# Recurrent layers of a four-layer decoder: sigmoids through ScalarE with a bounded input, one level product a quarter, key products one level ahead

## What is computed

```python
proj = h @ w_in                                   # 1024 x 4096
q, f, i, g = jnp.split(proj, 4, axis=-1)
q = jax.nn.silu(heads(q)); f = heads(f); v = heads(i)      # 8 heads of 128
log_f = jnp.logaddexp(jnp.log(lb), jnp.log1p(-lb) + jax.nn.log_sigmoid(f))
k = (1.0 - lb) * jax.nn.sigmoid(-f)
# o[t] = sum over s <= t of (q[t] . k[s] . prod of exp(log_f) over s < r <= t) v[s]
o = gla_chunkwise(q, k, v, log_f)
o = rmsnorm(o, head_norm)
return (o * jax.nn.silu(g)) @ w_out
```

## Time and profile before

| | us |
|---|---|
| median of three runs (1212.9 to 1214.92) | 1213.76 |
| the profiled execution | 1213.17 |
| its span, first to last instruction | 1211.0 |

### The profile page before, as it was taken

One profiled execution on the slowest core, in us unless ns is written; L12 is line 12 of the kernel. 1 busy time (PEld: TensorE's weight loads), 2 busy tenths in 40 slices (PEclk: granted clock), 3 DMA queues, 4 the chain that ended last, 5 costly groups with the idle time before them and its releaser, 6 DMA issues.

```text
span 1211.0 us, 16960 instructions
## 1 busy us (share of the span) xinstructions
PE 1156.7 (96%) x6750; PEld 1027.2 (85%) x6750; DVE 787.0 (65%) x825; ACT 639.9 (53%) x741; POOL 37.2 (3%) x53
## 2 busy tenths in 40 slices
PE   9778999999999999999999999999876999999998
PEld 8767999888889989888888888888875899888886
DVE  6567778655656676756657866555656787755663
ACT  6544566544454445645556654545653376544553
POOL 1110000000001000000000000000201000000000
PEclk9878999999999999999999999999987999999999
DMA  9322435565455644664654556456422343555450
GB/s 334 106 92 83 139 109 200 179 208 208 162 207 166 199 156 134 205 218 150 218 187 168 181 183 219 152 208 209 138 72 88 105 156 105 174 208 209 151 212 35
DMA packets 85960, 200.82 MB, mean 166 GB/s; under 512 B 3341, under 2 KB 6503, under 8 KB 85904
## 3 DMA queue, kind: packets, MB, share of 16 engines
q1 hardware_dynamic: 85872, 200.01, 48.4%
q0 software_dynamic: 32, 0.03, 0.0%
HBM read 198.95 MB, written 1.08 MB: 165 GB/s over the span
## 4 chain that ended last, share of the span: by engine, by line
PE 80%; DVE 8%; ACT 7%; issue 5%; POOL 0%; DVEq 0%; ACTq 0%; POOLq 0%
PE misc L625 10%; PE hb L625 10%; PE acc L677 10%; PE acc L678 10%; PE acc L679 10%; PE hb L630 5%; PE misc L630 5%; PE hb L569 3%; PE hb L571 3%; PE hb L572 3%; ACT whi L1048 3%; PE acc L832 1%; DVE arena L1661 1%; DVE wlo L1427 1%; PE misc L572 1%
## 5 line engine op out<-in xcount | busy, mean ns | idle before, releaser
L1427 DVE TENSOR_TENSOR wlo<-raw,whi 128x2048 fp32r<-128x2048 f32 x184 | 416.9, 2292 | 185.8 <-ACT whi L1048 184.6
L1048 ACT ACTIVATE whi<-raw 128x2048 fp32r<-128x2048 f32 x183 | 342.4, 1904 | 122.7 <-PE acc L679 104.8
L677 PE MATMUL acc<-whi,arena_r 128*128 128x512 f32 x512 | 199.9, 390 | 0.0
L678 PE MATMUL acc<-wlo,arena_r 128*128 128x512 f32 x512 | 199.5, 390 | 0.0
L679 PE MATMUL acc<-whi,arena_r 128*128 128x512 f32 x512 | 199.2, 389 | 0.0
L569 PE MATMUL hb<-xhl,whi 128*128 128x256 f32 x416 | 128.0, 308 | 7.6 <-DVE gains L1719 4.2
L625 PE MATMUL misc<-xhl,whi 128*128 128x512 f32 x512 | 122.6, 390 | 0.1
L625 PE MATMUL hb<-xhl,whi 128*128 128x512 f32 x512 | 122.7, 390 | 0.0
L571 PE MATMUL hb<-xhl,whi 128*128 128x256 f32 x416 | 122.6, 295 | 0.0
L572 PE MATMUL hb<-xhl,wlo 128*128 128x256 f32 x416 | 122.5, 294 | 0.0
L679 PEld LDWEIGHTS acc<-whi,arena_r 128*128 128x128 f32 x512 | 96.1, 188 | 20.2
(11 more groups left out here) (250 smaller groups left out, 1629.5 us busy)
## 6 DMA issues: line engine op xcount, KB each, us to landing
raw<-in_mlp_w_dram SPq DMA_DIRECT2D x128, 1024.0 KB, 5.4
raw<-in_a_w_in_dram SPq DMA_DIRECT2D x31, 1024.0 KB, 5.4
raw<-in_b_w_qkv_dram SPq DMA_DIRECT2D x12, 1024.0 KB, 6.8
raw<-in_a_w_out_dram SPq DMA_DIRECT2D x8, 1024.0 KB, 5.1
raw<-in_b_w_out_dram SPq DMA_DIRECT2D x4, 1024.0 KB, 5.1
arena<-in_x_dram SPq DMA_DIRECT2D x2, 512.0 KB, 4.6
raw<-in_a_w_in_dram SPq DMA_DIRECT2D x4, 256.0 KB, 4.3
arena<-bias_rows SPq DMA_DIRECT2D x1, 1024.0 KB, 10.8
```

What stands on the lines that cost most here:

```text
L677: pe.matmul(o, ys, h, start=first and kt == 0, stop=False, skip_group_check=True)
L678: pe.matmul(o, ys, l, start=False, stop=False, skip_group_check=True)
L1048: act.activation(whi[:, g % 2, u, 0:n], raw[:, g % 2, u, 0:n], ACT.Copy).then_inc(hi_done, 1)
L1427: dve.tensor_tensor(wlo[:, g % 2, u, 0:n], raw[:, g % 2, u, 0:n], whi[:, g % 2, u, 0:n].bitcast(F32), ALU.subtract).then_inc(lo_done, 1)
```

## The change

- The sigmoids are made by ACT alone, out of exp(-ln(1 + exp(-z))). So that exp cannot overflow, DVE bounds z to 40 in one `tensor_scalar` right behind the evict (`f_bound`, and inside `q_evict` and `gate_evict`). For f ACT makes six activations in one go (`sigmoids`; eight in layer 3), for q and the gate three (`silu`), and one DVE multiply follows for q and gate. The two DVE instructions of `f_b` are gone; those of `silu_a` and `gate_silu_a` became the bound.
- One level a quarter: `level_after` puts level l after quarter l + 3.
- In quarter q DVE first does the queries' product of the next level, then the keys' product of the level after that (one level ahead), then `select`; evictions, silu multiplies and the split follow.
- ACT's splits stand first in every even quarter, DVE's last in every odd one.
- The copy of levels 0 and 8 moves from DVE to ACT (`first_level`).
- PE makes the diagonal products of quad 1 a quarter earlier, the outputs of quad 0 after quarter 13 (before 17), the first sums of squares after 17 (before 20). In layer 0 its wait for the gains stands at level 0 (before: ahead of quarter 0).

The diff, cut:

```diff
+SATURATED = 40.0
...
-        after_quarter = {2: (0,), 3: (1,), 5: (2,), 6: (3,), 8: (4,), 9: (5,), 10: (6,), 11: (7, 8), 12: (9,), 13: (10,),
-                         14: (11,), 15: (12,), 16: (13,), 17: (14,), 18: (15,)}
+        def level_after(quarter):
+            return quarter - 3 if 3 <= quarter <= 18 else None
...
                         group("T", g0 + 1, 2, free, need, first_norm)
-                        pe.wait_ge(gains_sb, 2)
...
+                        elif level == 0 and layer == 0:
+                            pe.wait_ge(gains_sb, 2)
...
-                        pe.wait_ge(bank_free, free_count(layer) + 10)
+                        pe.wait_ge(bank_free, free_count(layer) + 8 + 2 * quad)
...
-                    also = {2: lambda: diagonal_products(0), 11: lambda: diagonal_products(1), 17: lambda: quad_outputs(0),
-                            20: lambda: (quad_outputs(1), oms_step(0), oms_step(1)),
+                    also = {2: lambda: diagonal_products(0), 10: lambda: diagonal_products(1), 13: lambda: quad_outputs(0),
+                            17: lambda: (oms_step(0), oms_step(1)), 20: lambda: quad_outputs(1),
                             22: lambda: (oms_step(2), oms_step(3))}
                     def some_steps(quarters=[0]):
                         if quarters[0] in also:
                             also[quarters[0]]()
-                        for level in after_quarter.get(quarters[0], ()):
-                            level_product(level)
+                        if level_after(quarters[0]) is not None:
+                            level_product(level_after(quarters[0]))
...
-                    def f_a(b):
-                        if b < 2:
-                            act.wait_ge(f_z, 2 * j + b + 1)
...
-                    def f_b(b):
-                        after_dve()
-                        for region in (ff, kq):
...
+                    def sigmoids(b):
+                        act.wait_ge(f_z, 4 * j + b + 1)
+                        z = scratch[b % 2][0].rearrange("p (t x) -> p t x", t=TT)
+                        own = [(bank_of(ff, b), -1.0), (bank_of(kq, b), 1.0)]
+                        for to, sign in own:
+                            ch.did(act.activation(to.rearrange("p t h x -> p t (h x)"), z, ACT.Exp, scale=sign))
...
+                            ch.settle(1)
+                            ch.did(act.activation(flat, flat, ACT.Ln, bias=1.0))
+                        for last, (to, _) in enumerate(own):
+                            ch.settle(1 - last)
...
+                                ins = act.activation(flat, flat, ACT.Exp, scale=-1.0)
...
-                    def silu_a(b):
-                        act.wait_ge(bank_free, free_count(layer) + (1, 2, 5, 6)[b])
-                        ln_1p_exp(bank_of(qq, b).rearrange("p t h x -> p t (h x)"),
-                                  scratch[b % 2][0].rearrange("p (t x) -> p t x", t=TT))
...
+                    def silu(i):
+                        act.wait_ge(silu_z, 8 * j + i + 1)
+                        if i >= 2:
+                            act.wait_ge(silu_done, 8 * j + i - 1)
+                        to = scratch[i % 2][1]
+                        if i < 4:
+                            z = bank_of(qq, i).rearrange("p t h x -> p t (h x)")
+                            ch.did(act.activation(to.rearrange("p (t x) -> p t x", t=TT), z, ACT.Exp, scale=-1.0))
...
+                            ch.did(act.activation(to, gz[i - 4], ACT.Exp, scale=-1.0))
+                        ch.settle()
+                        ch.did(act.activation(to, to, ACT.Ln, bias=1.0))
+                        ch.settle()
+                        act.activation(to, to, ACT.Exp, scale=-1.0).then_inc(sig_done, 1)
...
+                    def first_level(quad):
+                        act.wait_ge(g_mm, 16 * j + 8 * quad + 1)
+                        if quad:
+                            act.wait_ge(part_done, 2 * j + 1)
+                        act.activation(cmb, acc[2][:, :].rearrange("p (h x) -> p h x", h=4), ACT.Copy).then_inc(g_read, 1)
...
-                    f_a(0)
+                    out0 = first_group[f"out{layer}"]
                     split_unit(g0 + 2, 0, free=j + 1)
-                    f_a(1)
-                    f_b(0)
+                    sigmoids(0)
                     split_unit(g0 + 2, 1)
-                    f_b(1)
-                    silu_a(0)
-                    silu_b(0)
-                    out0 = first_group[f"out{layer}"]
+                    sigmoids(1)
+                    silu(0)
                     for quarter in range(24):
+                        if quarter % 2 == 0:
+                            split_unit(g0 + 3 + quarter // 4, quarter // 2 % 2)
+                        if quarter in (4, 12):
+                            first_level(quarter // 8)
+                        level = level_after(quarter)
+                        if level is not None and 1 <= (level + 1) % 8 < 7:
+                            k_pick(level + 1)
...
                         if quarter == 0:
-                            silu_a(1)
-                        if quarter in (2, 4):
-                            f_a(1 + quarter // 2)
-                        if quarter in (6, 8):
-                            silu_a(quarter // 2 - 1)
-                        if quarter % 2 == 0 and quarter < 22:
-                            split_unit(g0 + 3 + quarter // 4, quarter // 2 % 2)
-                        if quarter == 0:
-                            silu_b(1)
-                        if quarter in (2, 4):
-                            f_b(1 + quarter // 2)
-                        if quarter in (6, 8):
-                            silu_b(quarter // 2 - 1)
+                            silu(1)
                         if quarter == 1:
                             k_pick(0)
                         if quarter == 10:
                             k_pick(8)
-                        for level in after_quarter.get(quarter, ()):
-                            if level % 8 < 6:
-                                k_pick(level + 1)
...
+                        if quarter in (2, 4):
+                            sigmoids(1 + quarter // 2)
+                        if quarter in (6, 8):
+                            silu(quarter // 2 - 1)
...
-                    def f_b(b):
-                        a, z = (w.rearrange("p (t x) -> p t x", t=TT) for w in scratch[b % 2])
-                        f, k = tokens_of(ff, b), tokens_of(kq, b)
-                        after_act()
+                    def f_evict(b):
...
-                        ch.did(dve.scalar_tensor_tensor(out=f, in0=z, scalar=0.0, in1=a, op0=ALU.min, op1=ALU.subtract))
-                        ch.settle()
-                        turn(dve.tensor_tensor(k, f, z, ALU.subtract))
+                        ch.did(dve.tensor_scalar(scratch[b % 2][0], scratch[b % 2][0], -SATURATED, SATURATED,
+                                                 ALU.max, ALU.min), f_z)
...
+                    def q_evict(b):
                         k = (2, 3, 6, 7)[b]
                         dve.wait_ge(bank_ready, b0 + k + 1)
...
-                    def silu_a(b):
-                        a = scratch[b % 2][0].rearrange("p (t x) -> p t x", t=TT)
-                        after_act()
                         ch.settle()
-                        turn(dve.scalar_tensor_tensor(out=a, in0=tokens_of(qq, b), scalar=0.0, in1=a,
-                                                      op0=ALU.min, op1=ALU.subtract))
-                    def silu_b(b):
-                        a = scratch[b % 2][0].rearrange("p (t x) -> p t x", t=TT)
-                        after_act()
+                        z = tokens_of(qq, b)
+                        ch.did(dve.tensor_scalar(z, z, -SATURATED, None, ALU.max), silu_z)
+                    def q_silu(b):
+                        dve.wait_ge(sig_done, 8 * j + b + 1)
                         ch.settle()
-                        ch.did(dve.tensor_tensor(tokens_of(qq, b), tokens_of(qq, b), a, ALU.mult), silu_done)
...
                     def select(level):
                         dve.wait_ge(g_mm, 16 * j + level + 1)
...
+                        if level % 8 == 1:
+                            dve.wait_ge(g_read, 14 * j + 7 * (level // 8) + 1)
                         ch.settle()
-                        if level % 8 == 0:
-                            ch.did(dve.tensor_copy(cmb, gb), g_read)
-                        else:
-                            ch.did(dve.copy_predicated(cmb, over_heads(masks[:, level % 8, :]), gb), g_read)
+                        ch.did(dve.copy_predicated(cmb, over_heads(masks[:, level % 8, :]), gb), g_read)
...
-                    f_a(0)
-                    f_a(1)
+                    f_evict(0)
+                    f_bound(0)
+                    f_evict(1)
+                    f_bound(1)
                     split_unit(g0 + 2, 0)
...
-                    split_unit(g0 + 2, 1)
...
```

(35 more changed lines are left out.)

171 lines of the change are left out of this document (71 added, 100 removed).

## The result

| | before | changed |
|---|---|---|
| median of 4 runs each, us | 1213.43 (1212.90 to 1214.92) | 1148.18 (1146.93 to 1148.64) |
| span of the profiled execution, us | 1211.0 | 1146.5 |
| mean granted clock | 0.974 | 0.997 |

What follows compares the result with a forecast made beforehand. Idle PE and a low clock in two recurrent stages, from DVE's list order, were taken as the loss. Per stage 95.5 us plus waits (2.9, 3.7) and clock (2.4) gave 100.8 and 101.6, so 1155 us, range 1142 to 1178.

Steps and rivals of the forecast that it cites:

- What bounds it: Recurrent stages of layers 0 and 3: idle PE and low clock from DVE's list order; at most 35.0 and 35.1 us to gain.
- The ideal of 95.5 us a stage: PE's time for one recurrent stage if nothing waits, against 130.5 us before; the same in both layers.
- Part 1: First quarter of the stage: the 4.2 us wait ahead of quarter 0 and the low clock behind it go; no wait left.
- Part 2: Level products against DVE's list: product 5 waits 1.5 us before margins, product 9 0.4; sums 2.9 (layer 0), 3.7 us (layer 3).
- the sign: Expected in the changed profile: product 5, after quarter 8, waits 2 to 4 us for the queries at L1623.
- Part 3: ACT's list in the stages: extra copies and activations, and the weight loads, cost PE nothing.
- Part 4, the clock: Behind product 5's wait of 2.5 to 3.3 us the clock falls to half, costing 2.4 us a layer.
- rival B: Recurrent stages: waits shrink but the clock doesn't come back, 2 x 10.2 us lost, 1175 us; chance 0.05.
- Sum: Ideal, waits and clock per stage: layer 0 100.8 us, layer 3 101.6, gains of 29.7 and 29.0; 1155 us in all.
- A (DVE the bound): DVE arrives late at each level, 14.2 instead of 2.9 us a layer, 22.6 us worse, 1178 us; chance 0.18.
- C: Slower: at 12 splits a layer DVE still waits 3.8 us for ACT's queued copy, 1235 us; chance 0.03.
- D: Level products were late for PE's own reasons and stay so, no gain, 1213 us; chance 0.02.

Runs made afterwards that it cites:

- the best version: Changed kernel with quad 1's tree after product 5 and q's last eviction between the queries of level 5 and the keys of level 6: 1144.2 us.

## Why the prediction was right, point by point

- **What bounds it.** Right: both stages had lost by the order of DVE's list. The ideal of 95.5 us a stage stands up: at full clock PE was busy 96.0 us in layer 0, and 95.9 and 96.0 in the two layers of the best version. The single sizes were off in both directions. A T quarter with its product takes 3.84 us early in the stage (52.62 to 56.46), not 3.76; a W quarter with one takes 3.63 (72.87 to 76.50).
- **Part 1.** Right: PE doesn't wait ahead of quarter 0. The six activations took 3.2 us (26.21 to 29.45) where 3.7 was the bound, the split ends at 33.58, forecast 34.3, needed at 35.1.
- **Part 2.** The step held and the terms were too large. Product 5 is the one that waits, product 9 doesn't, and in quarters 5 to 9 DVE never waits for a copy. In layer 0 the wait was 0.85 us, though, below the 2 to 4 that I had named as the sign. In layer 0 I had the queries of level 5 done 33.9 us after quarter 0 without POOL, and they end at 69.04, which is 33.9, with it. But product 5 was due 33.2 us after quarter 0, not 32.4, by the longer T quarters and the 0.25 us at product 3 (my end of product 0, 14.4, was 0.2 above what its own terms add up to; it came at 14.5), and POOL cost 0.35 us (0.55 instead of 0.43 and 0.92 instead of 0.69), not 1.0. So 1.1 us in all instead of 2.9. In layer 3, 2.7 instead of 3.7; there POOL did cost 1.1 us, as the rows above show. The bound took 0.43 us, against 0.45 taken.
- **Part 3.** Right: no wait of PE in the stages is put down to ACT. The undone parts show how near it was: a delay in ACT's list was paid by PE at once, through the split's copy in one case and v's in the other.
- **Part 4, the clock.** This term was three times too large. I took 2.4 us a layer for both. In layer 0 the wait was 0.85 us and the clock stayed at 1.00. In layer 3 it fell in the profiled run, and PE's busy time there was 97.11 us, against 95.55 in a run of the same kernel where it stayed: 1.6 us. Together 1.6 instead of 4.8. Behind a wait of the same length it came in one of the two executions and not in the other, as the last section shows. And my rows of before were too few: beside the waits of 1.7, 4.2 and 5.6 us in the earlier trace rows, the same trace has falls behind 1.64, 1.91, 2.92, 3.37 and 3.87 us. So my reading of that trace at rival B, that the clock fell only behind waits of over 4 us, is wrong.
- **Sum.** Layer 0: 96.0 + 1.1 + 0 = 97.1, forecast 100.8. Layer 3: 95.5 + 2.7 + 1.6 = 99.8, forecast 101.6. The 5.5 us between are the clock (3.2), the waits (2.8), less 0.5 for PE's own time. Another 0.3 lies ahead of layer 0's stage, 0.4 outside the span and 0.6 in the medians, which makes the 6.8 us between 1155 and 1148.2. Nothing came back elsewhere: 705.9 us lie between the two stages, as before.
- **Rivals.** A (DVE the bound) was a fair fear for four quarters and no more; its sum took 2.9 us off in both layers where layer 3 had 3.7, 0.8 us too much in the 1178. B (the clock doesn't come back) didn't happen: the clock was 1.00 and 0.98. C didn't either, but its mechanism appeared when the split was put back early. D: the chain named in the earlier trace rows was the right one.

What I had not seen when I predicted is how the parts hang together: the forecast was for all of them at once, and the split alone shows that it wouldn't have held for one. Undone singly they cost 27 (split), 23 (sigmoids of f and q), 10 (keys) and 0 us (table). That this comes near 65 is no division of the gain: the same split brought only 5 alone. I haven't run the sigmoids, the keys or the table alone in the kernel before; what they bring there by themselves is open. So is how much of the 65 us the other changed places hold (the gate's steps, the gains' wait, the copy of levels 0 and 8). The traces give an estimate for one of them, the start of the stages: the waits ahead of quarter 0, 4.2 us in layer 0 and 3.4 in layer 3, are gone, and with them 5.3 and 6.0 us of PE's work at half clock, which cost 2.7 and 3.0 us. That makes some 13 us, but no run takes it by itself.

## What to carry to other kernels

An engine that is late though it is idle a third of the time is in the wrong place of its list: find the instruction before which it idles, and put it behind the work that others wait for. Do such edits together, since one alone may only uncover the next wait (the late split: 27 us undone, 5 us alone), and after each move ask what now stands behind it on that engine and on the one that it feeds. Once nothing in the list waits, a late operand needs less work in the stretch ahead of it. Here that was done by moving one eviction behind it and by starting GpSimd's tree later, both to places with slack. Where the splits were moved, the wait went from this operand to another one.

## What the runs showed of the hardware

**Behind middling waits the clock falls in some executions and not in others.** The same kernel, the same wait of PE, in two executions: the window behind the wait of 2.72 us, and that behind 2.66 us in the repeat.

```profile
873.30:878.18 4.88, 4.88 (x19) 4.05 (x20) 4.57 (x7) 4.09 (x5) 0.00 (x0) 0.65 0.51 187
```

```profile
873.56:878.44 4.88, 4.88 (x30) 4.36 (x31) 4.56 (x7) 4.08 (x5) 0.00 (x0) 1.00 0.50 186
```

In the first the 2.4 GHz were lost for some 3.5 of 4.9 us, in the second never. It fits that the five runs of the changed kernel beside the best one lie at 1146.5 and 1147.0 or at 1148.5 to 1148.7, two groups some 1.8 us apart, about the price of one fall. Over the recurrent stages of all traced kernels, before and after, of the waits that began at full clock none up to 1.56 us brought it down. Those from 1.6 to 2.8 us did in some cases and not in others: it fell behind 1.60, 1.64, 1.89, 1.91, 1.99, 2.72, 2.73 and 2.80, and stayed behind 1.66, 1.68, 1.70, 1.74, 1.86, 1.96, 2.10, 2.36, 2.37, 2.66 and 2.75 (a pair of 1.78 and 2.43 close together brought it down too, and isn't counted). All twenty of 2.9 us and more did. What decides within the band isn't shown here; the length of the wait doesn't. So in an estimate such a wait is better counted with a share of the price, here some 0.8 of 1.6 us, than as a yes or no; and to cut a wait from 2.7 to 1.5 us is worth more than the 1.2.

**VectorE and GpSimd hold each other up, by about a whole instruction.** Beside DVE's split, which ran from 56.05 to 58.33, POOL's first operation of the tree took 2.90 us in layer 0, and 1.04 in layer 3, where it started 0.03 us ahead of DVE's queries:

```profile
56.33 2.90 POOL L2001 TENSOR_TENSOR tree<-hn 128x512 f32<-128x512 f32 x1 [18.28 <-ACT arena L1154]
```

```profile
865.01 1.04 POOL L2001 TENSOR_TENSOR tree<-hn 128x512 f32<-128x512 f32 x1 [24.59 <-DVE hn L1567]
```

There it was the queries that took 1.56 us instead of 0.69, which is 0.87 more, near the 1.01 us that POOL's operation still had to run. The Trainium skill, "SBUF — State Buffer", section "Who interferes with whom", says that a VectorE instruction with two inputs in SBUF contends with a GpSimd instruction that reads SBUF. It calls the shared ports an exclusive lock, and says of VectorE's two-port modes that whoever issues first gets them for the whole instruction while the other is blocked. The trace fits that on both sides, for instructions with two inputs: POOL's 2.90 us are 2.00 until the split's end at 58.33 and 0.90 more, near its 1.04; and in both cases the engine that started later lost. The later tree moved that loss to product 6, where there was slack; beside a moved split it was longer there (2.93 us for POOL's first operation, 1.53 for the queries), and product 6 waited.
